# Sums of the activation halves on VectorE in nine passes, and another order of the seven products of a block

## What is computed

```python
h = _rms(x, norm_g[i])                  # 512 x 2048
u = h @ w_in[i]                         # 2048 x (9*1024 + 2*2048)
(hq, hi, hf_fwd, hf_bwd, hgate, nq, nk, nv, ngate, m_a, m_b) = jnp.split(u, _SPLITS, axis=-1)
...
y = jax.nn.sigmoid(m_a) * ya + jax.nn.sigmoid(m_b) * yb
x = x + y @ w_out[i]
```

## Time and profile before

| | |
|---|---|
| median of 3 runs | 1855.34 us (1855.1 to 1855.83) |
| the profiled execution, its own time | 1855.21 us |
| its span, first to last instruction | 1853.5 us |
| mean granted TensorE clock | 0.997 |
| PE busy | 1818.0 us (98%) |
| DVE busy | 1120.9 us (60%) |
| ACT busy | 828.7 us (45%) |
| POOL busy | 218.6 us (12%) |

### The profile page before, as it was taken

One profiled execution on the slowest core, in us unless ns is written; L12 is line 12 of the kernel. 1 busy time (PEld: TensorE's weight loads), 2 busy tenths in 40 slices (PEclk: granted clock), 3 DMA queues, 4 the chain that ended last, 5 costly groups with the idle time before them and its releaser, 6 DMA issues.

```text
span 1853.5 us, 25707 instructions
## 1 busy us (share of the span) xinstructions
PE 1818.0 (98%) x9521; PEld 1561.3 (84%) x9521; DVE 1120.9 (60%) x1322; ACT 828.7 (45%) x1137; POOL 218.6 (12%) x208
## 2 busy tenths in 40 slices
PE   6799999999999999999999999999999999999998
PEld 5699999888888888888888888888888888888887
DVE  6877777576776767667676666865544422244332
ACT  6244444554736547365473654734322232234221
POOL 6100000030211303113030120301000000000000
PEclk9899999999999999999999999999999999999999
DMA  6234433532323333232332332334555534465332
GB/s 208 71 109 135 145 118 98 146 91 86 91 83 92 91 91 91 84 91 87 94 91 79 91 96 85 91 105 132 162 150 147 169 124 165 163 238 182 126 128 77
DMA packets 291908, 217.80 MB, mean 118 GB/s; under 512 B 8825, under 2 KB 254616, under 8 KB 290320
## 3 DMA queue, kind: packets, MB, share of 16 engines
q1 hardware_dynamic: 288384, 205.04, 36.3%
q0 software_dynamic: 3472, 12.05, 1.9%
HBM read 192.45 MB, written 24.61 MB: 117 GB/s over the span
## 4 chain that ended last, share of the span: by engine, by line
PE 94%; DVE 3%; ACT 1%; issue 1%; DMA 1%; SPq 0%; DVEq 0%; ACTq 0%
PE mm_ps L1645 16%; PE mm_ps L1647 16%; PE mm_ps L1646 16%; PE mm_ps L1858 4%; PE mm_ps L1857 4%; PE mm_ps L1856 4%; PE ax_ps L1634 2%; PE ax_ps L1633 2%; PE ax_ps L1632 2%; PE ax_ps L1646 2%; PE ax_ps L1645 2%; PE ax_ps L1647 2%; PE mm_ps L1632 2%; PE ax_ps L1858 2%; PE ax_ps L1857 2%; PE ax_ps L1856 2%
## 5 line engine op out<-in xcount | busy, mean ns | idle before, releaser
L330 DVE TENSOR_TENSOR w_lo<-w_raw,w_hi 128x1024 fp32r<-128x1024 f32 (+1 forms) x232 | 316.2, 1363 | 500.0 <-ACT w_hi L321 498.8
L321 ACT ACTIVATE w_hi<-w_raw 128x1024 fp32r<-128x1024 f32 (+1 forms) x232 | 262.2, 1131 | 652.5 <-PE mm_ps L1647 350.2
L1645 PE MATMUL mm_ps<-act_hi,w_hi 128*128 128x512 f32 x1216 | 485.6, 399 | 0.0
L1647 PE MATMUL mm_ps<-act_hi,w_lo 128*128 128x512 f32 x1216 | 474.6, 390 | 0.0
L1646 PE MATMUL mm_ps<-act_lo,w_hi 128*128 128x512 f32 x1216 | 474.0, 390 | 0.0
L1647 PEld LDWEIGHTS mm_ps<-act_hi,w_lo 128*128 128x128 f32 x1216 | 228.2, 188 | 49.0
L1646 PEld LDWEIGHTS mm_ps<-act_lo,w_hi 128*128 128x128 f32 x1216 | 228.7, 188 | 44.9
L1645 PEld LDWEIGHTS mm_ps<-act_hi,w_hi 128*128 128x128 f32 x1216 | 228.6, 188 | 44.6
L1856 PE MATMUL mm_ps<-w_hi,act_hi 128*128 128x512 f32 x384 | 149.9, 390 | 0.0
L817 ACT ACTIVATE q_hi<-q_raw 128x1024 fp32r<-128x1024 f32 x84 | 86.4, 1055 | 141.9 <-DVE q_raw L1168 123.0
L1858 PE MATMUL mm_ps<-w_lo,act_hi 128*128 128x512 f32 x384 | 149.4, 389 | 0.0
(11 more groups left out here) (274 smaller groups left out, 3300.4 us busy)
## 6 DMA issues: line engine op xcount, KB each, us to landing
w_raw<-in_w_in SPq DMA_DIRECT2D x152, 512.0 KB, 3.7
q_raw<-in_w_in SPq DMA_DIRECT2D x56, 512.0 KB, 4.7
w_raw<-in_w_ple_gate SPq DMA_DIRECT2D x20, 768.0 KB, 4.2
w_raw<-in_w_out SPq DMA_DIRECT2D x16, 768.0 KB, 4.2
w_raw<-in_w_branch_a SPq DMA_DIRECT2D x16, 512.0 KB, 3.9
w_raw<-in_w_branch_b SPq DMA_DIRECT2D x16, 512.0 KB, 3.8
g_ab<-gate_dram SPq DMA_DIRECT2D x14, 512.0 KB, 4.3
gate_dram<-c_out SPq DMA_DIRECT2D x12, 512.0 KB, 5.2
```

The costliest lines, as they stand in the source:

```text
L321: nc.scalar.activation(w_hi[:, s, 0:width], w_raw[:, s, 0:width], ACT.Copy).then_inc(hi_done, 1)
L330: nc.vector.tensor_tensor(w_lo[:, s, 0:width], w_raw[:, s, 0:width], w_hi[:, s, 0:width].bitcast(F32), ALU.subtract).then_inc(lo_done, 1)
L1645: MM(bank, wh, m_hi[:, k0 + k, :], start=start and k == 0, stop=False)
L1647: mm = MM(bank, wl, m_hi[:, k0 + k, :], start=False, stop=stop and k == kn - 1)
```

## The change

The activation sums leave POOL. DVE makes all four in nine passes, in another order: S3 in `t2` (three passes: hi00 - hi10, + lo00, - lo10), S2 in `t1` as A11 - S3 (two passes), S1 in `t2` as S2 + A00 (two passes), S4 in `t1` as A01 - S2 (two passes). The splits of the sums follow in the order S3, S2, S1, S4. In a block the products are put in another order: 0: A00 with quarter 0; 1: A01 with the raw quarter below it (loaded second now); 2: S1; 3: S2; 4: A11; 5: S3; 6: S4. So the weight sums belong to the products 2, 3, 4 and 5; the one for 2 is made on DVE right behind the low split of product 0. Evictions and the bounds of their waits move with them: product 1 is evicted behind the low split of 4, products 3 and 2 behind that of 6. `act_hi` and `act_lo` become two halves of one tensor, and `s_hl` holds the high and the low part of a K tile side by side. The number of matmuls, weight splits, weight sums, evictions and loads is the same.

```diff
-            s_hl = sb("s_hl", [P, 4, 2, 8, S // 2], F32R, where=pre)
+            s_hl = sb("s_hl", [P, 4, 8, 2, S // 2], F32R, where=pre)
...
-        P_SIDE = [acts(0, 0), (s_hl[:, 0, 0], s_hl[:, 0, 1]), (s_hl[:, 1, 0], s_hl[:, 1, 1]), acts(0, 1),
-                  acts(1, 1), (s_hl[:, 2, 0], s_hl[:, 2, 1]), (s_hl[:, 3, 0], s_hl[:, 3, 1])]
-        P_SUMS = {1: 1, 2: 2, 5: 3, 6: 4}
-        P_QUARTER = [0, 0, 0, 3, 3, 1, 2]
-        Q_DONE = [4, 5, 6, 4]
-        T_COUNT = {1: 1, 2: 2, 4: 3, 5: 4}
+        P_SIDE = [(0, 0), (0, 1), 1, 2, (1, 1), 3, 4]
+        S_COUNT = {3: 1, 2: 2, 1: 3, 4: 4}
+        P_QUARTER = [0, 1, 0, 0, 1, 2, 3]
+        Q_DONE = [4, 4, 5, 6]
+        T_COUNT = {2: 1, 3: 2, 4: 3, 5: 4}
...
-                k, j = (0, 0, 1, 1)[l], (0, 1, 1, 0)[l]
+                k, j = (0, 1, 0, 1)[l], (0, 0, 1, 1)[l]
...
-            hi_11, lo_11 = acts(0, 0)
-            hi_21, lo_21 = acts(1, 0)
-            pool.wait_ge(h_lo, 2 * KT)
-            T = nc.gpsimd.tensor_tensor
-            T(t2[:, :, :], hi_11.bitcast(F32), hi_21.bitcast(F32), ALU.subtract).then_inc(s3_sum, 1)
-            pool.wait_ge(s3_sum, 1)
-            T(t2[:, :, :], t2[:, :, :], lo_11.bitcast(F32), ALU.add).then_inc(s3_sum, 1)
-            pool.wait_ge(s3_sum, 2)
-            T(t2[:, :, :], t2[:, :, :], lo_21.bitcast(F32), ALU.subtract).then_inc(s3_sum, 1)
-
...
-            def sum_hi(n, t):
-                A(s_hl[:, n, 0], t[:, :, :], ACT.Copy).then_inc(s_hi_done, 1)
+            def sum_hi(n, t, done):
+                act.wait_ge(s_sum, done)
+                A(s_hl[:, n - 1, :, 0], t[:, :, :], ACT.Copy).then_inc(s_hi_done, 1)
 
             plain_hi(act, 3)
             plain_hi(act, 4)
             plain_gate(0)
-            act.wait_ge(s_sum, 3)
-            sum_hi(0, t1)
             plain_hi(act, 5)
+            sum_hi(3, t2, 3)
             plain_hi(act, 6)
             plain_gate(1)
-            act.wait_ge(s_sum, 5)
-            sum_hi(1, t1)
             plain_hi(act, 7)
+            sum_hi(2, t1, 5)
...
                         if is_first and b == 0 and u == 0:
                             plain_gate(2)
-                            act.wait_ge(s3_sum, 3)
-                            sum_hi(2, t2)
-                            act.wait_ge(s_sum, 7)
-                            sum_hi(3, t1)
+                        if is_first and b == 0 and u == 1:
+                            sum_hi(1, t2, 7)
                         if is_first and b == 0 and u == 2:
                             plain_gate(3)
+                            sum_hi(4, t1, 9)
...
-                                act.wait_ge(p_evict, r * 21 + (7 * (b - 1) + 3))
+                                act.wait_ge(p_evict, r * 21 + (7 * (b - 1) + 2))
...
-            t = t1[:, :, :]
+            v1, v2 = t1[:, :, :], t2[:, :, :]
             plain_lo(dve, 3)
-            half_sum(0, HALF["hi10"], HALF["hi11"], ALU.add)
             plain_lo(dve, 4)
-            half_sum(1, t, HALF["lo10"], ALU.add)
-            half_sum(2, t, HALF["lo11"], ALU.add)
+            half_sum(0, v2, HALF["hi00"], HALF["hi10"], ALU.subtract)
+            half_sum(1, v2, v2, HALF["lo00"], ALU.add)
             plain_lo(dve, 5)
-            sum_lo(0, 0, t1)
-            half_sum(3, t, HALF["hi00"], ALU.subtract)
-            half_sum(4, t, HALF["lo00"], ALU.subtract)
+            half_sum(2, v2, v2, HALF["lo10"], ALU.subtract)
+            half_sum(3, v1, HALF["hi11"], v2, ALU.subtract)
             plain_lo(dve, 6)
+            half_sum(4, v1, v1, HALF["lo11"], ALU.add)
+            sum_lo(3, v2, 1)
             plain_lo(dve, 7)
-            sum_lo(1, 1, t1)
-            half_sum(5, HALF["hi01"], t, ALU.subtract)
-            half_sum(6, t, HALF["lo01"], ALU.add)
+            dve.wait_ge(s_lo_done, 1)
+            half_sum(5, v2, v1, HALF["hi00"], ALU.add)
+            sum_lo(2, v1, 2)
...
-                o, x, y, q = {1: (0, 1, 0, 1), 2: (0, 2, 0, 2), 4: (3, 3, 0, None), 5: (1, 2, 1, None)}[u]
+                o, x, y, q = {2: (0, 2, 0, 2), 3: (0, 3, 0, 3), 4: (1, 1, 0, None), 5: (2, 3, 2, None)}[u]
...
-                if u == 2:
+                if u == 1:
                     dve.wait_ge(p1_ready, r * 3 + (b + 1))
-                    TT(u_2[:, :], p_bank(2), p_1[:, :], ALU.add).then_inc(p_evict, 1)
-                    dve.wait_ge(p_evict, done + 1)
-                    TT(u_4[:, :], p_bank(1), u_2[:, :], ALU.add).then_inc(p_evict, 1)
-                if u == 3:
                     if not isinstance(r, int) or r > 0:
                         dve.wait_ge(c_stored[b % 3], r * 16)
-                    TT(c[:, 0, lo], p_bank(3), p_1[:, :], ALU.add).then_inc(p_evict, 1)
+                    TT(c[:, 0, lo], p_bank(1), p_1[:, :], ALU.add).then_inc(p_evict, 1)
+                if u == 3:
+                    TT(u_2[:, :], p_bank(3), p_1[:, :], ALU.add).then_inc(p_evict, 1)
+                    dve.wait_ge(p_evict, done + 2)
+                    TT(u_4[:, :], p_bank(2), u_2[:, :], ALU.add).then_inc(p_evict, 1)
...
                         pre_lo(r, b, u)
                         if u in (1, 2) and not (is_first and b == 0):
                             evict(r, b - 1, u + 4)
+                        if u in (4, 6):
+                            evict(r, b, u - 3)
                         if is_first and b == 0 and u == 0:
-                            sum_lo(2, 2, t2)
+                            half_sum(6, v2, v2, HALF["lo00"], ALU.add)
                         if is_first and b == 0 and u == 1:
-                            sum_lo(3, 3, t1)
-                        if u in (5, 6):
-                            evict(r, b, u - 3)
-                        if u + 1 in T_COUNT:
+                            dve.wait_ge(s_lo_done, 2)
+                            half_sum(7, v1, HALF["hi01"], v1, ALU.subtract)
+                            sum_lo(1, v2, 3)
+                            half_sum(8, v1, v1, HALF["lo01"], ALU.add)
+                        if u == 0:
+                            weight_sum(r, b, 2)
+                        if u + 1 in T_COUNT and u != 1:
                             weight_sum(r, b, u + 1)
+                        if is_first and b == 0 and u == 2:
+                            sum_lo(4, v1, 4)
...
-            FREED = {1: 5, 2: 1, 3: 3, 4: 6, 5: 4, 6: 7}
+            FREED = {1: 1, 2: 5, 3: 2, 4: 6, 5: 4, 6: 7}
```

More of the change, by code:

```diff
@@ L122, in build_kernel @@
         sb("to_2k", [P, 24])
-        act_hi = sb("act_hi", [P, KT, S], F32R)
-        act_lo = sb("act_lo", [P, KT, S], F32R)
+        act_hl = sb("act_hl", [P, 2, KT, S], F32R)
+        act_hi, act_lo = act_hl[:, 0], act_hl[:, 1]
         reset = sb("reset", [P, S])
@@ L234, in build_kernel @@
         g_out_stored = [sem("g_out_stored0"), sem("g_out_stored1")]
-        s_sum, s3_sum, s_hi_done, s_lo_done = (sem(n) for n in ("s_sum", "s3_sum", "s_hi_done", "s_lo_done"))
+        s_sum, s_hi_done, s_lo_done = (sem(n) for n in ("s_sum", "s_hi_done", "s_lo_done"))
         x_ready = [sem(f"x_ready{t}") for t in range(NT)]
@@ L335, in acts, with p_side @@
             return tuple(a[:, 8 * j:8 * j + 8, i * (S // 2):(i + 1) * (S // 2)] for a in (act_hi, act_lo))
-        P_SIDE = [acts(0, 0), (s_hl[:, 0, 0], s_hl[:, 0, 1]), (s_hl[:, 1, 0], s_hl[:, 1, 1]), acts(0, 1),
-                  acts(1, 1), (s_hl[:, 2, 0], s_hl[:, 2, 1]), (s_hl[:, 3, 0], s_hl[:, 3, 1])]
-        P_SUMS = {1: 1, 2: 2, 5: 3, 6: 4}
-        P_QUARTER = [0, 0, 0, 3, 3, 1, 2]
-        Q_DONE = [4, 5, 6, 4]
-        T_COUNT = {1: 1, 2: 2, 4: 3, 5: 4}
+        P_SIDE = [(0, 0), (0, 1), 1, 2, (1, 1), 3, 4]
[3 more added lines that the diff above has]
+        T_COUNT = {2: 1, 3: 2, 4: 3, 5: 4}
+        def p_side(u, k):
+            if isinstance(P_SIDE[u], int):
+                return s_hl[:, P_SIDE[u] - 1, k]
+            i, j = P_SIDE[u]
+            return act_hl[:, :, 8 * j + k, i * (S // 2):(i + 1) * (S // 2)]
         def p_num(r, b, u):
@@ L1128, in _, with half_sum, sum_lo @@
                     for n, v in zip((f"hi{i}{j}", f"lo{i}{j}"), acts(i, j))}
-            def half_sum(n, a, b, op):
+            def half_sum(n, o, a, b, op):
                 if n:
                     dve.wait_ge(s_sum, n)
[L1133 to L1137, removed]
-            t = t1[:, :, :]
+                TT(o, a, b, op).then_inc(s_sum, 1)
+            def sum_lo(n, t, done):
+                dve.wait_ge(s_hi_done, done)
+                TT(s_hl[:, n - 1, :, 1], t, s_hl[:, n - 1, :, 0].bitcast(F32), ALU.subtract).then_inc(s_lo_done, 1)
+            v1, v2 = t1[:, :, :], t2[:, :, :]
             plain_lo(dve, 3)
-            half_sum(0, HALF["hi10"], HALF["hi11"], ALU.add)
             plain_lo(dve, 4)
-            half_sum(1, t, HALF["lo10"], ALU.add)
-            half_sum(2, t, HALF["lo11"], ALU.add)
+            half_sum(0, v2, HALF["hi00"], HALF["hi10"], ALU.subtract)
+            half_sum(1, v2, v2, HALF["lo00"], ALU.add)
             plain_lo(dve, 5)
-            sum_lo(0, 0, t1)
```

(35 more changed lines are left out.)

## The result

The changed kernel takes 1839.68 us (median of 4, 1839.31 to 1840.12) against 1855.40 us for the kernel before beside it (4 runs, 1855.1 to 1855.83). The ratio is 0.9914, 95% interval 0.9901 to 0.9926. The forecast was 1839.7 us, range 1836.5 to 1844.5. The profiled execution took 1839.31 us, its span is 1837.6 us.

A forecast was written before the change was run, and what follows sets the result against it. PE, busy 98%, was taken as the bound, losing 18.5 us mostly waiting for DVE's low splits. With 3.0 us remaining, 15.5 us come off the profiled 1855.21 us, 1839.7 us against the median; range 1836.5 to 1844.5 us.

The forecast's parts named there:

- The account of the 18.5 us: PE's loss before the heads: waits 13.4, restarts 0.8, half clock 3.4, product 2 hiccups 0.9 us; 3.0 us would remain.
- the stretch: PE from plain unit 2 at 39.19 us to the heads' first matmul at 332.32: 293.1 us, 274.6 of it work.
- POOL as the cause of the late VectorE: While POOL makes S3, 17.4 us of DVE time hold 4.7 us of work; 12.7 us lost to POOL.
- The layout of the first stretch: DVE's queue through block 0: product 3's low split at 80.4 to 81.6 us; PE waits 1.0, 0.6, 0.9 us.
- The blocks: New order in the blocks: DVE's round falls from 20.23 to 19.0 us, no stall, 0.9 us come back.
- the hiccup at product 2: Steady blocks: product 2's second matmul follows after 0.20 us instead of 0.12, its low split late; 0.9 us over 11 blocks.
- this rival: Product 5 bounds each block if its three chains, cover 0.5 us, are each 0.27 us longer: 1843.9 us, chance 0.08.
- The load: Quarter 2, wanted one product earlier: 6.9 us from free to wanted, landing 4.7 us, 2.2 us to spare, no cost.
- the slower rival: Quarter 2's load lands too late, each further us recurring in 11 blocks; at about 10 us, 1859 us; chance 0.03.
- The layout in SBUF: DVE passes writing low parts in rows with gaps: bounds -0.1 and +0.1 us for four passes, taken as 0.
- the fall of the clock: Granted clock falls once more behind the three waits at 81 to 89 us, costing 1.7 us: 1841.4 us, chance 0.10.

The follow-up runs named there:

- sums alone: Kernel before with the changed kernel's sums (nothing on GpSimd, nine VectorE passes), old product order, weight sums, evictions and layout kept: 1843.78 us, ratio 0.9935.

## Why the prediction was right, point by point

- **The account of the 18.5 us** held: 15.7 us less in the stretch, 2.8 left, forecast 3.0. It was made from start to start of matmuls and not from busy shares, which showed 98% and 99%. The terms agree within 0.4 us (waits of 2.1 us for 2.5, 2.8 us lost for 3.0), so the agreement of 1839.68 with 1839.7 us is closer than the working deserves; that much is luck.
- **POOL as the cause of the late VectorE**: shown by putting its passes back (12.75 us) and by taking them out of the old kernel (12.1 us by the medians, 11.2 by the heads' first matmul). The forecast said 12.7 us of VectorE time; put back, the passes make VectorE 12.6 us late. How much of that reaches PE, as waits and as half clock, is another sum.
- **The layout of the first stretch**: forecast for the low split of product 3 80.4 to 81.6 us, in the trace 80.61 to 81.83, in a trace in which plain unit 2 starts 0.26 us later than in the kernel before. Waits forecast 1.0, 0.6, 0.9 us, measured 1.07, 0.29, 0.78. From start to start the last two cost 0.51 us (81.98 to 85.37, less 2.88) and 1.03 us (85.37 to 89.28), so 0.22 to 0.25 us over the idle in the row, where the forecast added 0.16. The clock stayed at 1.00 behind them.
- **The blocks**: the hiccup at product 2 is gone. From 89.28 us, the first matmul of product 5 of block 0, to 316.87 PE does 79 products in 227.6 us, 2.881 each, so nothing is lost there. Product 5 is next, as forecast, with a cover of 0.4 us rather than 0.5. The experiments with more VectorE work show this rival's price; it was real and near.
- **The load**: from release to wanted 6.9 us (in the changed kernel's trace from 266.46, the end of the low split of product 4, to 273.33, the start of the weight sum), as laid out. What was mis-sized is the landing, 4.1 us and not 4.7, so the room is 2.8 us and not 2.2. The price of the slower rival also holds: lateness past the cover comes back in every block, 12.4 us for 1.14 us more.
- **The layout in SBUF**: the low parts, written with gaps, take 2.29 us for 2.28. Nothing, as taken.
- **What was missed**: the fall of the clock was priced only as a rival for the changed kernel, where it did not come. In four experiments PE waited 2 us and more at once and the clock fell: passes back on GpSimd, copies on GpSimd, no passes on GpSimd, sums alone. It stands in none of the four expectations. Shorter waits than laid out made up for it in the first and the last; with no passes on GpSimd the heads started 1.6 us late by it; for the copies the forecast was only a range, 5 to 12 us.

## What to carry to other kernels

An engine at 12% use can still be the cause: look at the durations of the same instruction form in two stretches, and at what else ran when it was three or four times longer. A cheap-looking offload to GpSimd of passes that read SBUF can cost VectorE nearly the whole length of each, as here, where VectorE's passes beside them have two inputs; the fills cost nothing. Account for a PE-bound stretch from start to start, lay the new queue out with the durations of the trace, and find the next chain and its cover in the same step: slack in an engine's round is not the slack of a chain that a ring of buffers starts anew.

## What the runs showed of the hardware

- A VectorE instruction with two SBUF inputs waits for the end of a GpSimd instruction that reads SBUF: +1.5 to 1.7 us beside one-input copies whatever its own length, +4.2 to 4.4 us beside two-input passes, the first of which takes 4.61 us. Fills of 1.86 us cost it nothing.
- The granted clock fell from 1.00 to 0.50 (1.2 of 2.4 GHz) behind single waits of PE that differ little from others behind which it stayed: it fell behind 2.16 us (copies on GpSimd), behind 2.63 us (sums alone) and behind 2.00 and 2.59 us (no passes on GpSimd), and stayed behind 1.02 and 2.58 us in the kernel before (the row below, right behind the 2.58). Between 39 us and the start of the heads no run had it fall behind waits of 1.1 us or less alone. What tells the cases apart wasn't tried.

```profile
96.00:98.00 2.00, 2.00 (x19) 2.00 (x18) 1.86 (x2) 0.11 (x1) 0.00 (x0) 1.00 0.03 9
```
